# First FFN product of an fp32 encoder layer: one 512-column matmul for high and low activations, sums chained in banks, and the fourth weight sum moved to GpSimd

## The reference, cut to what matters

```python
gu = rmsnorm(h, g_pre_ffn) @ w_ffn_in          # (tokens, 2048) @ (2048, 2 * 5632)
g, u = jnp.split(gu, 2, axis=-1)
h = h + rmsnorm((jax.nn.silu(g) * u) @ w_ffn_out, g_post_ffn)
```

## Time and profile before

| | us |
|---|---|
| median of 3 runs (2728.43 to 2729.52) | 2728.7 |
| the profiled execution's own time | 2728.66 |
| its span, first to last instruction | 2726.5 |
| granted TensorE clock over the span, share of full speed | 0.998 |
| TensorE busy | 2694.1 |
| VectorE busy | 1946.7 |
| ScalarE busy | 1086.7 |
| GpSimd busy | 338.1 |

### The profile page before, as it was taken

The page is one execution under the profiler, slowest core; times in us unless marked ns, Lnnn a source line. Parts: engine busy times, 40 slices in busy tenths (PEclk is TensorE's granted clock), DMA queues, the critical chain, the costliest instruction groups (busy, mean ns, idle before and its releaser), DMA issues.

```text
span 2726.5 us, 41873 instructions
## 1 busy us (share of the span) xinstructions
PE 2694.1 (99%) x16358; PEld 2416.1 (89%) x16358; DVE 1946.7 (71%) x2269; ACT 1086.7 (40%) x1413; POOL 338.1 (12%) x205
## 2 busy tenths in 40 slices
PE   8999999999999999999999999999999999999997
PEld 7999888888888888878999999999999888888886
DVE  7888655555554432276999999999998888886524
ACT  7333333333334422253444444444444444444422
POOL 0000000000000000000244344343433000000000
PEclk9999999999999999999999999999999999999999
DMA  6433522222225544253444434344346755544322
GB/s 257 155 117 117 150 91 77 77 82 88 77 89 152 148 152 146 94 187 121 171 144 146 154 142 167 133 155 164 123 173 258 259 187 183 214 167 153 139 93 108
DMA packets 174237, 396.15 MB, mean 145 GB/s; under 512 B 17846, under 2 KB 52014, under 8 KB 171566
## 3 DMA queue, kind: packets, MB, share of 16 engines
q1 hardware_dynamic: 149120, 340.99, 36.6%
q10 hardware_dynamic: 25006, 53.60, 5.1%
HBM read 336.81 MB, written 57.73 MB: 145 GB/s over the span
## 4 chain that ended last, share of the span: by engine, by line
PE 85%; issue 10%; DMA 1%; DVE 1%; ACT 1%; SPq 0%; POOL 0%; DVEq 0%; POOLq 0%
PE bank L2339 10%; PE bank L2337 10%; PE bank L2338 10%; PE bank L2178 8%; PE bank L2179 8%; PE bank L2180 8%; PE bank L2417 5%; PE bank L2418 5%; PE bank L2419 5%; PE bank L2586 4%; PE bank L2588 4%; PE bank L2589 4%; PE bank L2211 1%; DMA x_f<-xT 1%; DMA o_a_first<-w_ffn_pieces 0%
## 5 line engine op out<-in xcount | busy, mean ns | idle before, releaser
L2337 PE MATMUL bank<-act_hi,w_hi 128*128 128x256 f32 x1664 | 471.2, 283 | 2.4 <-DVE act_lo L1449 1.4
L2338 PE MATMUL bank<-act_lo,w_hi 128*128 128x256 f32 x1664 | 470.9, 283 | 0.0
L2339 PE MATMUL bank<-act_hi,w_lo 128*128 128x256 f32 x1664 | 470.9, 283 | 0.0
L844 ACT CAST w_hi<-w_raw 128x1024 fp32r<-128x1024 f32 x210 | 211.7, 1050 | 585.3 <-PE bank L2180 326.6
L1358 DVE TENSOR_TENSOR w_lo<-w_raw,w_hi 128x1024 fp32r<-128x1024 f32 x208 | 246.5, 1222 | 244.3 <-ACT w_hi L844 244.3
L2337 PEld LDWEIGHTS bank<-act_hi,w_hi 128*128 128x128 f32 x1664 | 319.4, 192 | 2.9 <-DVE act_lo L1449 1.6
L2338 PEld LDWEIGHTS bank<-act_lo,w_hi 128*128 128x128 f32 x1664 | 319.5, 192 | 0.1
L2339 PEld LDWEIGHTS bank<-act_hi,w_lo 128*128 128x128 f32 x1664 | 319.5, 192 | 0.0
L2178 PE MATMUL bank<-act_hi,w_hi 128*128 128x512 f32 x752 | 296.2, 394 | 0.3 <-DVE w_lo L1358 0.3
L2179 PE MATMUL bank<-act_lo,w_hi 128*128 128x512 f32 x752 | 293.1, 390 | 0.0
L2180 PE MATMUL bank<-act_hi,w_lo 128*128 128x512 f32 x752 | 293.0, 390 | 0.0
(11 more groups left out here) (293 smaller groups left out, 5952.5 us busy)
## 6 DMA issues: line engine op xcount, KB each, us to landing
w_raw<-w_in SPq DMA_DIRECT2D x92, 512.0 KB, 4.0
w_a_even<-w_ffn_in SPq DMA_DIRECT2D x80, 512.0 KB, 4.3
xop<-xop_dram SPq DMA_DIRECT2D x35, 1024.0 KB, 11.5
w_a_odd<-w_ffn_in SPq DMA_DIRECT2D x60, 512.0 KB, 4.7
xop_dram<-h_sums ACTq DMA_DIRECT2D x20, 1024.0 KB, 6.4
o_a_odd<-w_ffn_pieces SPq DMA_DIRECT2D x40, 512.0 KB, 7.7
o_a_even<-w_ffn_pieces SPq DMA_DIRECT2D x39, 512.0 KB, 6.9
w_raw<-w_ffn_in SPq DMA_DIRECT2D x36, 512.0 KB, 5.2
```

The source lines that it names most:

```text
L2337: nc.tensor.matmul(out, w_hi[:, slot, k], hi, start=k == 0, stop=False)
L2338: nc.tensor.matmul(out, w_hi[:, slot, k], lo, start=False, stop=False)
L2339: last = nc.tensor.matmul(out, w_lo[:, slot, k], hi, start=False, stop=k == HALF - 1)
```

## The change

Four things, all in the pair stage:

- **TensorE**: the high and the low activations now lie in one tile (`act_both`), and `d1`, `t2`, `d2` already did. One 512-column matmul takes the high weights with high and low activations side by side (result: 512 columns, whose two halves have to be added later), and one 256-column matmul takes the low weights with the high activations. That is 8 x 2 matmuls per product in place of 8 x 3.
- **Chained banks**: products of a pair are added up in three banks (`PAIR_BANKS`, taken in turns by even and odd pairs) instead of one bank each. ScalarE copies a bank at six points of a pair (`keep_chain`): one copy of bank to bank and three of 512 columns to SBUF, and two of 256 columns, so that the low half of a bank can be added to its high half. TensorE waits for such a copy (`kept`) before products 2, 4 and 6.
- **VectorE** does six `combine`s per pair in place of seven: four of 256 columns and two of 512, of which three have an operand in a bank and three have both in SBUF. They stand a product later than before (`finish_up` and `finish_hidden` of a pair fall into products 0 and 1 of the next).
- **The fourth weight sum** goes from VectorE to GpSimd (`fourth_sum`), between GpSimd's operand work; ScalarE waits for it (`out_four`) before the high part of product 5.

Around the stage, banks and counts of the output stage and of the tail are renamed to fit. The core of the diff:

```diff
+SUMS_FFN = 4 * GATE_PAIRS + 1
+SUMS_OUT = SUMS_FFN + 3 * PAIRS
+FIRSTS_OUT = GATE_PAIRS
+COMBINED_FFN = GATE_PAIRS * PRODUCTS
+PAIR_BANKS = ((0, 1, 5), (2, 3, 4))
+PAIR_CHAIN = (0, 1, 2, 0, 2, 1, 2)
+COPIES = 6
...
+        act_both = at("act_both", R_X, [P, 2, KT, T], F32R)
+        act_hi, act_lo = act_both[:, 0], act_both[:, 1]
...
+        low_half = at("low_half", R_S + 5 * KB, [P, S])
+        second_kept = at("second_kept", R_Q + 48 * KB, [P, 2, S])
+        up_kept = at("up_kept", R_Q + 52 * KB, [P, 2, S])
+        third_kept = at("third_kept", R_Q + 54 * KB, [P, 2, S])
```

GpSimd:

```diff
                                         ALU.subtract).then_inc(h_lo_ready, 1)
 
-            def operands(i, first=False):
-
+            def fourth_sum(n, par):
+
+                a11, a12, _, _ = w_four[par]
+                pool.wait_ge(w_summed, n * 3 + (SUMS_FFN + 3))
+                pool.wait_ge(lo_ready, n * PRODUCTS + (GATE_PAIRS * PRODUCTS + H_SEVEN + 1 + 3))
+                pool.wait_ge(four_landed[par][1], n * 8 + (GATE_PAIRS * 8 + 16 - 8 * par))
+                nc.gpsimd.tensor_tensor(w_sum, a11, a12, ALU.add).then_inc(out_four, 1)
+
+            def low_of_sums(i):
+                pool.wait_ge(h_summed, i * SUMS + SUMS)
+                pool.wait_ge(h_hi_ready, i * 3 + 3)
+                low_in_place(h_sums, slice(0, 4))
+
+            def operands(i, first=False, last=False):
+
+                fourth_sum(i * 2 + 1, 1)
+                if not first:
+                    low_of_sums(i + (-1))
                 pool.wait_ge(hid_ready, i * 2 + (CH + 1))
...
                 low_in_place(h_even, slice(0, 1))
+                if not last:
+                    fourth_sum(i * 2 + 2, 0)
```

ScalarE (`ffn_high`, `open_gate`, `high_of_hidden` and `high_of_sums` are the former lines as functions, with the fourth sum's wait on `out_four`):

```diff
+            def ffn_high(n, q, j, first):
+
+                par, (n_sum, kind) = q % 2, PRODUCT_FROM[j]
+                if n_sum == 4 and not first:
+                    act.wait_ge(out_four, n)
+                elif n_sum:
+                    act.wait_ge(w_summed, n * 3 + (SUMS_FFN + n_sum) if not first else GATE_PAIRS * 4 + n_sum)
+                else:
+                    act.wait_ge(four_landed[par][kind], n * 8 + (GATE_PAIRS * 8 + 16 - 8 * par))
+                src = w_sum if kind is None else w_four[par][kind]
+                nc.scalar.copy(w_hi[:, (H_SEVEN + GATE_PAIRS * PRODUCTS + PRODUCTS * q + j) % 4], src).then_inc(hi_ready, 1)
+
+            def keep_chain(n, q, j, first):
+
+                a, g, b = PAIR_BANKS[q % 2]
+                if j == 0:
+                    if not first:
+                        act.wait_ge(combined, n * COPIES + (COMBINED_FFN - COPIES))
+                    nc.scalar.copy(bank[:, b], bank[:, a]).then_inc(kept, 1)
+                elif j == 1:
+                    if not first:
+                        act.wait_ge(combined, n * COPIES + (COMBINED_FFN - COPIES + 2))
+                    nc.scalar.copy(second_kept[:].rearrange("p a t -> p (a t)"), bank[:, g]).then_inc(kept, 1)
+                elif j == 2:
+                    if not first:
+                        act.wait_ge(combined, n * COPIES + (COMBINED_FFN - COPIES + 5))
+                    nc.scalar.copy(third_kept[:].rearrange("p a t -> p (a t)"), bank[:, b]).then_inc(kept, 1)
+                elif j == 3:
+                    act.wait_ge(combined, n * COPIES + COMBINED_FFN)
+                    nc.scalar.copy(low_half[:], bank[:, a, S:]).then_inc(kept, 1)
+                elif j == 4:
+                    act.wait_ge(hid_ready, n + CH)
+                    nc.scalar.copy(up_kept[:].rearrange("p a t -> p (a t)"), bank[:, b]).then_inc(kept, 1)
+                elif j == 6:
+                    act.wait_ge(combined, n * COPIES + (COMBINED_FFN + 1))
+                    nc.scalar.copy(low_half[:], bank[:, b, S:]).then_inc(kept, 1)
...
-                            product_high(p0 + (GATE_PAIRS + q4), q4, j4, H_SEVEN)
+                            ffn_high(p0 + q4, q4, j4, first and q4 == 0)
...
+                            continue
+                        if j == 0:
+                            open_gate(f + (-1))
+                        if j == 2:
+                            high_of_hidden(f + (-1), q % 2 == 0)
+                        if q % 2 == 0 and j == 5:
+                            high_of_sums(r, q // 2)
+                        if q % 2 and j == 1 and not (first and q == 1):
                             store_sums(r, q // 2, r * 2 + (q // 2 - 1))
```

VectorE (`ffn_low` and `ffn_sum` are `product_low` and the first three cases of `weight_sum`):

```diff
+            def finish_up(n, q):
+                b = PAIR_BANKS[q % 2][2]
+                dve.wait_ge(kept, n * COPIES + COPIES)
+                dve.wait_ge(combined, n * COPIES + (COMBINED_FFN + 3))
+                combine(up_kept[:, 0], low_half[:], bank[:, b, 0:S])
+
+            def finish_hidden(n, q, stored, dst, sums_read):
+                f = n + CH
+                dve.wait_ge(combined, n * COPIES + (COMBINED_FFN + COPIES))
+                dve.wait_ge(silu_ready, f + 1)
+                if stored is not None:
+                    dve.wait_ge(h_stored[q % 2], stored)
+                    if sums_read is not None:
+                        dve.wait_ge(h_summed, sums_read)
+                nc.vector.scalar_tensor_tensor(dst[:, :, 1].bitcast(F32), up_kept[:], -1.0, gu[:], ALU.mult,
+                                               ALU.mult).then_inc(hid_ready, 1)
...
+                            dve.wait_ge(op_done, n * PRODUCTS + (COMBINED_FFN + 6))
+                            combined_before(2)
+                            combine(up_kept[:, 1], up_kept[:, 0], up_kept[:, 1])
+                            combine(both(third_kept), both(third_kept), bank[:, g])
                             combined_before(4)
...
-                            combined_before(2)
-                            combine(gu[:, 1], y_sum[:], product(5))
-                            combined_before(6)
-                            nc.vector.tensor_tensor(gu[:].rearrange("p a t -> p (a t)"), gu[:].rearrange(
-                                "p a t -> p (a t)"), rstd[:], ALU.mult).then_inc(ffn_read, 1)
-                        if j == 6:
-                            combine(up[:, 0], v_sum[:], product(6))
-                            combined_before(7)
-                            dve.wait_ge(silu_ready, f + 1)
-                            dst = (h_even, h_odd)[q % 2]
-                            if not (first and q < 2):
-                                dve.wait_ge(h_stored[q % 2], p0 * (8 + 8 * (q % 2)) + 16 * (1 + q % 2) * (q // 2))
-                                if q % 2 == 0:
-                                    dve.wait_ge(h_summed, p0 * (SUMS // 2) + SUMS * (q // 2))
-                            nc.vector.scalar_tensor_tensor(dst[:, :, 1].bitcast(F32), up[:], -1.0, gu[:], ALU.mult,
-                                                           ALU.mult).then_inc(hid_ready, 1)
-                        q4, j4 = q + (j + 4) // PRODUCTS, (j + 4) % PRODUCTS
-                        if not (last and q4 == 4):
-                            product_low(p0 + (GATE_PAIRS + q4), q4, j4, H_SEVEN)
-                        else:
-                            step_low(j4)
+                            combine(gu[:, 1], third_kept[:, 0], third_kept[:, 1])
+                            combined_before(5)
+                            nc.vector.tensor_tensor(both(gu), both(gu), rstd[:], ALU.mult).then_inc(ffn_read, 1)
+                        if 2 <= j <= 4 and not (last and q == 3):
+                            ffn_sum(n + 1, q + 1, j - 1)
                         if last and q == 3:
                             for which, i in SUM_FIRST.get(j, ()):
                                 out_sum(0, which, i)
+                        q4, j4 = q + (j + 4) // PRODUCTS, (j + 4) % PRODUCTS
```

TensorE:

```diff
+            def chained_product(n, q, j):
+
+                pe.wait_ge(lo_ready, n * PRODUCTS + (COMBINED_FFN + H_SEVEN + j + 3))
+                slot = (H_SEVEN + COMBINED_FFN + PRODUCTS * q + j) % 4
+                out = bank[:, PAIR_BANKS[q % 2][PAIR_CHAIN[j]]]
+                for k in range(HALF):
+                    parts = both_parts(j, k)
+                    nc.tensor.matmul(out.rearrange("p (a t) -> p a t", a=2), w_hi[:, slot, k], parts,
+                                     start=j < 2 and k == 0, stop=False, skip_group_check=True)
+                    last = nc.tensor.matmul(out[:, 0:S], w_lo[:, slot, k], parts[:, 0], start=False,
+                                            stop=k == HALF - 1, skip_group_check=True)
+                last.then_inc(op_done, 1)
+
+            def chain_free(n, j, first):
+
+                if j == 0 and not first:
+                    pe.wait_ge(combined, n * COPIES + (COMBINED_FFN - 2 * COPIES + 1))
+                if j == 1 and not first:
+                    pe.wait_ge(combined, n * COPIES + (COMBINED_FFN - 2 * COPIES + 4))
+                if j in (2, 4, 6):
+                    pe.wait_ge(kept, n * COPIES + (j - 1))
```

(5 more changed lines are left out.)

176 lines of the change are left out of this document (108 added, 68 removed).

## The result

The change makes the kernel slower: 2759.42 us median of 4 runs (2758.47 to 2761.9) against 2729.11 for the kernel before beside it (2728.43 to 2729.95), a ratio of 1.0113 [1.0099, 1.0126], +30.3 us. 2772 was predicted, with a range from 2710 to 2800. The profiled execution took 2758.47 us, its span is 2756.7, 30.2 more than before.

What follows compares the result with a forecast made beforehand. TensorE bounded, VectorE 5% behind; VectorE with GpSimd in its way would take over at 16.1 + 5.2 = 21.3 us per pair against 20.1: +48 over 40 pairs, less 5 for the lead, so 2728.7 + 43 = 2772 us, range 2710 to 2800.

Steps and rivals of the forecast that it cites:

- GpSimd's turns: Pair stage: GpSimd and VectorE instructions on SBUF operands exclude each other; VectorE loses 5.2 us per pair of GpSimd's 5.9.
- VectorE's own work: Pair stage: VectorE's work undisturbed by GpSimd falls from 17.3 to 16.1 us per pair.
- I take -0.1: Combining on VectorE in the pair stage: 4.25 us before, 4.40 now, less one instruction and a 0.21 us wait.
- The pair before: Pair stage: the old kernel's pair was taken as 20.1 us, so the change adds 1.2 us per pair, 48 over 40.
- The lead: ScalarE and VectorE work four products ahead of TensorE; using that up once takes about 5 us off the loss.
- it catches up, 0 to 2 us, taken as 0: Start of the output stage: VectorE, 86% busy there, makes up its lateness from the pair stage at no cost.
- I take the sum of the two: TensorE, pair stage: a 512- and a 256-column matmul cost 0.227 + 0.120 us, saving 0.72 us per pair, 29 us.
- rival A: TensorE stays the pair stage's bound, VectorE losing at most 3.3 us per pair to GpSimd: 2700 us, chance 0.14.
- ScalarE and DMA: Pair stage: ScalarE's copies add 2.7 us per pair, 11.9 in all, at no cost; DMA changes nothing in the loop.
- B: VectorE bounds but loses the same share to GpSimd as before, 3.9 us per pair: 2720 us (2712 to 2730), chance 0.14.
- C, the ring: Late VectorE and ScalarE hold each other up through TensorE, 0.4 to 1.0 us more per pair: 2788 to 2812, chance 0.13.
- D: 512-column matmuls miss the output stage's rate, each product staying at 2.88 us; alone, with low losses: 2729 us, chance 0.03.

Runs made afterwards that it cites:

- run 1: The changed kernel with the fourth weight sum back on VectorE, all else as changed: 2721.00 us, 0.9969 of the kernel before.
- run 3: The changed kernel with GpSimd's fourth weight sum computing only 8 of its 1024 columns, waits and order kept: 2718.09 us.
- run 4: The changed kernel with GpSimd's fourth weight sum cut into four instructions of 256 columns: 2735.02 us.
- 5: The changed kernel with GpSimd's fourth sum on 8 columns and each product's eight 512-column matmuls ahead of its eight 256-column ones: 2708.34 us.
- 6: The changed kernel with GpSimd's fourth sum on 8 columns and three 256-column matmuls again in place of one of 512 and one of 256: 2732.49 us.
- run 10: The changed kernel with only its matmuls grouped, eight of 512 columns and then eight of 256 per product: 2759.01 us.
- run 2: The kernel before the change with only the fourth weight sum moved from VectorE to GpSimd: 2759.95 us.

## Why the prediction was right, and where its sizes were off

**What bounds, and who takes over.** Right. TensorE bounded, VectorE was 5% behind, and VectorE with GpSimd in its way is the new bound: its share of the stage's middle is 98.7% (predicted over 98%), single low parts take 3.43 and 3.42 us (3.4), the mean low part 1.66 (335.4 us by 202 in the three groups above; 1.7), the fourth sum 2.70 (2.5 to 3.5), and TensorE's gap per cycle comes before product 3. TensorE's share is 95.5%, not 91%: a good third of its products ran at 0.353 us per couple and not at 0.347, and VectorE needed less per pair than predicted.

**GpSimd's turns.** Predicted 5.2 us lost per pair, measured 5.2. That it agrees to a tenth is luck: the bounds were 4.4 and 5.9, and the value between them was a judgement. That VectorE loses so much is not luck: run 1 shows it by taking the sum away (-38.4 us), run 3 by taking only its columns away (-41.3). It was not so exclusive as the prediction's bounds had it: both large instructions fell on VectorE whole, but of four small ones one slipped by (run 4). The Trainium skill (SBUF — State Buffer, Who interferes with whom) states that the two instructions exclude each other, and the traces agree: 3.43 us instead of 1.22 with both operands in SBUF, 0.68 unchanged with one in a bank. How the turns fall between short instructions made 24 us between the change and run 4.

**VectorE's own work: the term that was mis-sized.** Predicted 16.1 us per pair, and it is 20.96 - 5.24 = 15.7. The step that failed is the one on combining, "I take -0.1": it set durations against each other, where the distances between starts count. By these (the instructions on banks and halves, none of them disturbed, from 1474.89 to 1485.45 before and from 1610.85 to 1622.93 in the changed kernel), the combining of a pair with its `rstd` product and its `h` took 4.36 us before, where four sums were read by the very next instruction (0.45 us to it, 0.63 ahead of `h`), and takes 3.98 now: a 512-column one starts its follower after 0.60 (1592.32 to 1592.92), a 256-column one after 0.34 (1617.61 to 1617.95). That is -0.4, 0.3 us of the difference; 0.1 is left that I can't place. On VectorE's 20.96 in place of 21.3 us per pair hang 14 us.

**The pair before.** The sum set 21.3 against 20.1 us, the cycle of one window; over 38 pairs it was 20.20. Another 4 us.

**The lead.** Predicted 5 off, and it was 6.2, with the 2.0 us of "issue": 1 us. But it was not kept: nearly all of it is lost again in the output stage.

**The output stage.** Predicted 0 to 2 us, taken as 0: it was 5.9. The step that failed is "it catches up, 0 to 2 us, taken as 0": VectorE does not catch up, because it stands idle for 5.65 us, waiting for `o_a_first`, whose issue hangs on a low part that comes 30.1 us later while TensorE comes 24.2 later. Runs 1, 3, 5 and 6 pay this too: TensorE's output matmuls begin 1.9 to 3.8 us before `o_a_first` is issued (the kernel before: 1.0 after), VectorE is idle for it for 5.6 to 6.4 us, and TensorE waits 2.6 to 2.7 us for `acc`. VectorE has slack in the pairs of three of them, so it isn't lateness piled up over 40 pairs; that it comes of the new order, with the combining a product later, is argued, not shown, and no run moved the transfer.

The four together: +43 - 14 - 4 - 1 + 6 = +30, as measured.

**TensorE.** Predicted 0.72 us less per pair, 29 us; runs 3 and 6 give 0.37 per pair and 14.4 us. The step that failed is "I take the sum of the two" pure streams: 0.347 us per couple, where a stream without gaps takes 0.354 in alternation and 0.350 grouped. The changed kernel, with its gaps, does reach 0.347 in half of its products. Run 10 shows that the forecast did not hang on it; rival A did, whose time is 2718 (run 3) and not 2700. Per matmul saved that is 14.4/2240 = 6.4 ns, half of the 13 that the pure streams suggested. By the 2.5 ns that the Trainium skill (TensorE: Matmul & The Clock Gate, Back-to-back issue gap) gives for isolated matmuls it would have been 5.6 us, an estimate. The measurement lies between this and the 29.

**ScalarE and DMA.** Costed at nothing, and in the pair stage rightly: ScalarE is busy for 316.74 us in 28.6 pairs, 11.1 per pair (11.9 predicted), and no wait of TensorE there names it; the queues move 143 GB/s at a share of 0.40 (148 and 0.42 before). Behind the stage the transfer of `o_a_first` is not free, as said above.

**The rivals.** A needed at most 3.3 us lost, and 5.2 were; run 3 is the state that it describes. B (the same share lost as before) would have been 3.9. C, the ring, did not come: over the whole stage VectorE's waits for ScalarE are 2.9 us, where they were 15.7. Waits of that kind appear in run 2 instead. D (nothing gained from 512 columns) is out by run 6, though the gain is only half of what the pure rates promised.

## What to carry to other kernels

A sum of two SBUF operands moved from a nearly full VectorE to GpSimd is not taken off VectorE: here it saved 1.14 us of VectorE and put 2.3 into its way, so the move alone cost 38 us; look first at what such an instruction beside VectorE already does in the trace. If the work has to be on GpSimd, cut it to small instructions: that was worth 24 us here. Price a mixed stream of matmuls by a mixed stream, group matmuls of one width where TensorE bounds, and count an engine's work by the distances between starts. A lead that one engine uses up is not won if the next stage's transfers wait for the late engine: here 5.9 of 6.2 us came back.
